# One core, one transformer layer: moving GpSimd's norm gains and modulation rows, VectorE's low parts and the compressed softmax within the attention loop

## What is computed

```python
mod = silu(c) @ w_mod + b_mod                    # 6 x 2048: shift, scale, gate, twice
q   = rms_norm(heads(nsa_q), q_gain) * 64**-0.5  # 16 heads of 64, in 4 groups
# three branches, each softmax(q k - slope * distance) v, masked to the past:
o_c = softmax(q @ k_cmp, 31 compressed keys) @ v_cmp
o_s = softmax(q @ k_slc, all 8 blocks are picked) @ v_slc
o_w = softmax(q @ k_win, window 512) @ v_win
o   = g0 * o_c + g1 * o_s + g2 * o_w
x   = x + gate_a * (concat(pool, gla, o) @ w_out)
```

## Time and profile before

| what | us |
|---|---|
| median of 3 runs | 2626.35 |
| lowest and highest of them | 2625.59 and 2627.77 |
| the profiled execution | 2625.79 |
| its span from first to last instruction | 2623.9 |
| TensorE busy over the span | 2488.2 (95%) |
| VectorE, ScalarE, GpSimd busy | 893.6, 779.3, 1148.0 |
| the attention stage, 665 to 925 us | 260.0, TensorE busy 223.39 |

### The profile page before, as it was taken

One profiled execution on the slowest core, in us unless ns is written; L12 is line 12 of the kernel. 1 busy time (PEld: TensorE's weight loads), 2 busy tenths in 40 slices (PEclk: granted clock), 3 DMA queues, 4 the chain that ended last, 5 costly groups with the idle time before them and its releaser, 6 DMA issues.

```text
span 2623.9 us, 33211 instructions
## 1 busy us (share of the span) xinstructions
PE 2488.2 (95%) x11481; PEld 2028.5 (77%) x11481; DVE 893.6 (34%) x1413; ACT 779.3 (30%) x1482; POOL 1148.0 (44%) x894
## 2 busy tenths in 40 slices
PE   5589999999789999979999999999999999999999
PEld 3577777887688888858888888888888888888887
DVE  4765332258576677771202020201020202010102
ACT  2023224232456622233222222222222222222221
POOL 0024323444576634434444444444444444444443
PEclk8579999999799999989999999999999999999999
DMA  8742223365211177742232323322332332332333
GB/s 298 258 147 81 64 68 103 113 237 180 85 49 57 65 250 256 259 159 95 97 97 96 95 89 96 96 89 94 96 90 94 96 94 90 96 96 89 95 96 112
DMA packets 86221, 315.96 MB, mean 120 GB/s; under 512 B 9584, under 2 KB 10240, under 8 KB 84736
## 3 DMA queue, kind: packets, MB, share of 16 engines
q1 hardware_dynamic: 84240, 303.31, 35.5%
q10 hardware_dynamic: 1904, 11.62, 1.2%
HBM read 310.69 MB, written 4.19 MB: 120 GB/s over the span
## 4 chain that ended last, share of the span: by engine, by line
PE 63%; issue 24%; POOL 10%; DVE 2%; ACT 0%; POOLq 0%; ACTq 0%; DVEq 0%
PE ps L429 57%; POOL wlo L342 9%; PE ps L769 2%; PE ps L758 1%; PE ps L726 1%; PE ps L727 1%; DVE macc L1203 1%; POOL qn L362 0%; DVE biasT L1490 0%; PE ps L712 0%; PE ps L750 0%; POOL kn L367 0%; POOLq L341 0%; PE ps L741 0%; POOL pmod L385 0%
## 5 line engine op out<-in xcount | busy, mean ns | idle before, releaser
L342 POOL TENSOR_TENSOR wlo<-raw,whi 128x512 fp32r<-128x512 f32 x728 | 964.0, 1326 | 1365.5 <-ACT whi L894 1103.2
L894 ACT ACTIVATE whi<-raw 128x512 fp32r<-128x512 f32 x612 | 385.9, 632 | 1260.6 <-PE ps L429 1127.7
L429 PE MATMUL ps<-hfH,whi 128*128 128x512 f32 x1408 | 559.0, 397 | 17.1 <-DVE hfL L1620 13.1
L429 PE MATMUL ps<-hfL,whi 128*128 128x512 f32 x1408 | 558.8, 397 | 0.0
L429 PE MATMUL ps<-hfH,wlo 128*128 128x512 f32 x1408 | 558.3, 397 | 0.0
L429 PEld LDWEIGHTS ps<-hfH,whi 128*128 128x128 f32 x1408 | 266.5, 189 | 80.8 <-issue 13.9
L429 PEld LDWEIGHTS ps<-hfH,wlo 128*128 128x128 f32 x1408 | 266.4, 189 | 61.4
L429 PEld LDWEIGHTS ps<-hfL,whi 128*128 128x128 f32 x1408 | 266.6, 189 | 60.9
L1647 DVE SCALAR_TENSOR_TENSOR x1T<-ps,modc,x1T 128x512 f32<-128x512 f32 x176 | 132.1, 751 | 455.9 <-PE ps L429 455.9
L429 PE MATMUL ps<-huH,whi 128*128 128x512 f32 x704 | 279.2, 397 | 0.5 <-DVE huL L1631 0.5
L429 PE MATMUL ps<-huL,whi 128*128 128x512 f32 x704 | 279.1, 396 | 0.0
(11 more groups left out here) (262 smaller groups left out, 2926.7 us busy)
## 6 DMA issues: line engine op xcount, KB each, us to landing
raw<-in_wstream SPq DMA_DIRECT2D x370, 512.0 KB, 3.6
modw<-in_mstream SPq DMA_DIRECT2D x192, 512.0 KB, 4.6
xT<-in_xt SPq DMA_DIRECT2D x4, 1024.0 KB, 8.2
w1s<-in_w ACTq DMA_DIRECT2D x2, 2048.0 KB, 8.3
x1T<-in_xt ACTq DMA_DIRECT2D x4, 1024.0 KB, 8.6
out_y<-x1T SPq DMA_DIRECT2D x16, 256.0 KB, 2.0
cmpb<-in_cmp_tab ACTq DMA_DIRECT2D x1, 1024.0 KB, 7.1
ptab<-in_tabs ACTq DMA_DIRECT2D x1, 768.0 KB, 5.1
```

Of the source, the lines that this page charges most:

```text
L342: nc.gpsimd.tensor_tensor(wlo[:, s, :], raw[:, r, :], whi[:, s, :].bitcast(F32), ALU.subtract).then_inc(unit_ready, 1)
L429: ins = nc.tensor.matmul(acc, lhs, rhs, start=first and n == 0, stop=last and n == 2)
L894: A(whi[:, k % SPLIT, :], raw[:, k % 8, :], ACT.Copy).then_inc(unit_hi, 1)
```

## The change

GpSimd: the scaling of the queries moves from tile 3 to tile 2, and the gains of groups 2 and 3 from tiles 4 and 8 to tiles 3 and 7, ahead of that tile's modulation rows. The 48 rows are no longer three to a tile but follow a table. TensorE: the compressed values at n % 8 = 2, not 3. ScalarE: the exponentials of the compressed scores behind the copy of unit n, not ahead of it, and their transposed copy at 1, not 2. VectorE: `cmp_soft` at 2, not 0, `cmp_sum` at 5, not 3, and the low part five units behind its preparation step, not two, now ahead of the compressed work in a unit. No instruction is added or removed.

```diff
+        POOL_ROWS = (3, 5, 2, 0, 3, 5, 4, 0, 3, 5, 4, 2, 4, 5, 3, 0)
...
             for tile in range(T * G):
-                if tile == 3:
+                if tile == 2:
                     pool.wait_ge(rq_ready, 1)
...
-                if tile in (4, 8):
-                    gains(tile // 4 + 1)
-                for n in range(3 * tile, 3 * tile + 3):
+                if tile in (3, 7):
+                    gains(tile // 4 + 2)
+                for n in range(row_at, row_at + POOL_ROWS[tile]):
                     mod_row(n)
+                row_at += POOL_ROWS[tile]
                 add_branches(tile)
...
-                if n % 8 == 3 and tile:
+                if n % 8 == 2 and tile:
                     cmp_values(tile - 1)
...
+                if n < NU:
+                    save_pt(n)
                 if n % 8 == 0 and tile:
                     act.wait_ge(cs_ready, tile)
                     A(pc[:, :], sc[:, :], ACT.Exp, scale=-1.0).then_inc(cp_ready, 1)
-                if n < NU:
-                    save_pt(n)
-                if n % 8 == 2 and tile:
+                if n % 8 == 1 and tile:
                     act.wait_ge(cpt_psum, tile)
...
                 if n < NU:
                     reduce_scores(n)
-                if n % 8 == 0 and tile:
+                if 0 <= n - 5 < NU - 32 and (n - 5) % 32 in PREP_AT:
+                    prep_low((n - 5) // 32 + 1, PREP_AT.index((n - 5) % 32))
+                if n % 8 == 2 and tile:
                     cmp_soft(tile - 1)
-                if n % 8 == 3 and tile:
+                if n % 8 == 5 and tile:
                     cmp_sum(tile - 1)
...
-                if n // 32 + 1 < G and m - 2 in PREP_AT:
-                    prep_low(n // 32 + 1, PREP_AT.index(m - 2))
```

More of the change, by code:

```diff
@@ L404, in _ @@
             pool.wait_ge(mod_read, 13)
+            row_at = 0
             for tile in range(T * G):
-                if tile == 3:
+                if tile == 2:
                     pool.wait_ge(rq_ready, 1)
```

## The result

| kernel | runs | median us | lowest to highest |
|---|---|---|---|
| before | 4 | 2627.06 | 2625.59 to 2630.04 |
| changed | 4 | 2652.32 | 2651.03 to 2654.19 |

The ratio is 1.0095, with a 95% interval of 1.0079 to 1.0111: the change costs 25.3 us. The forecast was 2652.6 us. The profiled execution took 2651.03 us, with a span of 2649.1.

The account below looks back on a forecast made before the run. TensorE bounds the attention where not held up. Stalls +26.7, clock +18.9, port +2.0, waits for gains -12.4, slow stretches -5.5, copies -2.1, end -0.8 make +26.8 on 2625.79: 2652.6 us, range 2631 to 2670.

Parts of the forecast that it names:

- Stalls: TensorE's transposes at 18 preparation places wait for VectorE's low part: +26.7 us, from 24 to 28.3.
- the steps: Each place: 0.16 us, minimum's start 0.22, low part 0.69, TensorE's start 0.05, plus the minimum; 1.33 to 1.73 us.
- the two late places: First group, where TensorE already waited for VectorE's squares (2.50) and ScalarE's square root (2.35): 0.5 and 1.0 us added.
- the circle: Transposes wait for the low part, behind a minimum that waits for TensorE's just-issued scores; lead useless, 1.33 to 1.73 us each.
- rival 1: Clock holds behind the stalls: +7.9, 2633.7 us, chance 0.22; low half, stalls 24 and no port cost, 2629, 0.06.
- Clock: TensorE's clock falls behind 7 of 16 new idles in the attention, 2.7 us each: +18.9 us, from none to 48.
- Gains and the stretches behind them: GpSimd's earlier gains of groups 2 and 3 end two TensorE waits, 12.4 us, and slow stretches behind, 5.5 us.
- the port: Moved gains hold VectorE up in SBUF at two group boundaries, 1 us each: +2.0 us.
- Compressed part: Compressed softmax at later units: VectorE's 18.6 us wait goes, TensorE regains 2.1 us behind ScalarE's copies.
- End: At the attention's end VectorE no longer shares SBUF with three modulation rows: -0.8 us, between 0 and 1.5 off.
- rival 3: Low part is read before TensorE reaches the transposes, so no stall shows: -18.8, 2607 us; chance 0.07.
- Rival 2: Low clock stays, one slow stretch running into the next; 16 falls at 3.0 us: 2682 us; chance 0.07.

Follow-up runs that it names:

- filled: The changed kernel with five throwaway products on TensorE ahead of the transposes at each of the 18 places; 2635.27 us.
- the two experiments: Changed kernel with GpSimd's queue as before, 2667.0 us (14.7 above changed); kernel before with GpSimd's part alone, 2612.2 us (saves 15.5).
- only_compressed: The kernel before with only the compressed work moved to its new units, on three engines; 2620.04 us, ratio 0.9981.

## Why the prediction was right, and which terms were off

The forecast was +26.8 us on the profiled execution and the profiled one after is +25.2 above it. The mechanism, the signs and the places were right: 18 waits for low parts, sixteen of them 1.39 to 1.79 us (I had put 1.2 to 1.6) and the two late ones 3.51 and 4.20. But that the sum came so close is luck. The low part cost 49.7 us and not 45.6, and the compressed part saved 6.9 and not 2.1, and these two errors of 4 to 5 us cancel.

**Stalls: 26.7 forecast, too small.** The mechanism was as told. In the steps, start of the minimum (0.22) and the low part (0.69) held; TensorE starts 0.15 us behind its releaser, not 0.05, which I had read from a wait for GpSimd, and the places with queries are another 0.1 us longer. The visible idles in the second and third group are 1.39, 1.53, 1.66, 1.79, 1.75 and 1.39 us, 9.5 a group, where my steps less their 0.16 of overlap give 8.5. In the first group the idles are 14.2 us, of which 2.50 and 2.35 were there before, so 9.3 new, where I had 7.2. There the two late places (3.51 and 4.20 us) cost 1.0 and 1.9 more than the old waits, not 0.5 and 1.0: VectorE's late work and the circle added up almost fully. In sum 28.3 us of new idle against some 24.1 forecast. One bound was added up wrongly: with both late places at nothing the low end is 28.3 - 1.46 - 1.59 = 25.2 us, not 24, and the low half of rival 1 lies 1.2 us higher with it.

**Clock: 18.9 forecast, about 20 measured.** The size is nearly right by two errors. In the places outside the two that fell before, the clock fell 9 times, not 7. Those nine low stretches hold 47.35 - 3.25 - 3.40 = 40.7 us of work, 4.5 us each and not the 5 to 7 us of the earlier trace rows, since most are 3.4 us long. At half clock that is up to 2.3 us for each fall and not 2.7, 20.3 us in all; the filled idles give 20.1 by estimate, of which 17.0 came back as time. Net of what went with the gains the forecast was 13.4 us, and TensorE's busy time grew by 10.6. The difference is mostly the two late places, whose stretches now hold 6.65 us of work and not 12.93. The rule of the Trainium skill that I named, "TensorE: Matmul & The Clock Gate", section "Why this matters for your kernels", would have kept the clock at these idles of 1.4 to 1.8 us, and the runs do not agree: the clock fell behind nine of them, and filling the very same idles brought back 17.0 us.

**Gains and the stretches behind them: 17.9 less 2.0 for the port, plus 0.8 at the end.** Right: 14.7 and 15.5 us by the two experiments, against 16.7. TensorE's wait for `kn` went fully. The port's 2.0 us did not show at the two group boundaries: while the gains of group 2 ran, from 747.97 to 755.41, TensorE had one wait, 1.39 us up to 751.54, and at the same place of the last group, where no gains run, it is 1.39 us too (up to 882.25). Where the two engines do meet at a cost is at the start of the attention, in both kernels, which the prediction left out.

**Compressed part: 2.1 forecast, 2 to 8 measured.** The size was off and so was the reason. The copies' 2.1 us did go, but in the changed kernel three waits for `pc` bring 1.8 of them back. In the trace of only_compressed the gain is in the clock, but one execution doesn't show that the order of the work is what brings it.

**End: 0.8 forecast, 0.5 measured** in the wait for `q_tok` (3.4 to 2.9 us).

The rivals: rival 3 would have needed the wait for `kn` gone and none for the low parts, and the waits show 18. Rival 2 needed one slow stretch to run into the next, and only three of the eleven are longer than 3.4 us. Rival 1 is what filled shows, at 2635.3 us.

## What to carry to other kernels

When a step is moved later on one engine, write down what now stands ahead of it in that engine's queue and what that waits for: if it waits for work that the blocked engine has issued in the same unit, every lead is lost, and one unit closer brings most of it back (38.2 us here between five units and four, 49.7 between five and two). Price a short idle in a busy stage twice, once for itself (28.3 us here) and once for the slower work behind it (about 20 us here); where it can't be removed, throwaway work in it was worth 17.0 us. A change made of three parts can hold two good ones: run each alone before the whole is thrown away.

## What the runs showed of the hardware

In the changed kernel the granted clock fell to 0.50 behind nine of sixteen idles of TensorE of 1.39 to 1.79 us (in the 3.40 us ahead of one fall the engine was busy 2.33 us), and the low stretches were 3.4 or 6.8 us long. Behind idles of the same length in the wide units at the end of a group (1.75 and 1.39 us, up to 872.65 and 882.25) it did not fall, nor behind two idles of 1.32 and 1.33 us in filled (up to 796.96 and 856.70), where TensorE is busy with throwaway work just ahead.

Four operations of VectorE beside GpSimd's multiplications took 8.52 us in one execution, 3.24 us in another, of kernels that don't differ there, and 2.05 us with GpSimd held back. Where they were long, GpSimd's four key gains took 2.8 us, and where they were short, 3.5. So how two engines meet at SBUF can vary between executions by more than many a change is worth, and either of the two can be the one that waits. The spread of before (2618.5 to 2629.43 over 17 runs) is of that size; that it has this cause was not shown, since only the profiled executions have a trace. The Trainium skill, "SBUF — State Buffer", section "SBUF: two separate sides", tells of the lock between the two engines; these times agree with one that holds now VectorE and now GpSimd.
